# A mixture-of-experts loop: a turn of four experts instead of eight, and the down bias as a combination of its own

## The chip, the cores and the metric

One core of one Trainium2 chip runs the whole program. The metric is the device time of one execution in microseconds (us).

## The reference

One inference step of a decoder trunk of one layer, for 256 prompt tokens and 8 sample tokens (264 together), model width 1024, all in float32. Ahead of the part that changes stand a mixer and a cross-attention. Then comes a mixture of 32 experts, of which each token takes 4:

```python
def expert_ffn(xb, w1, b1, w2, b2):
    gu = xb @ w1 + b1                       # 1024 -> 2048
    gate, up = gu[:, :D_EXPERT], gu[:, D_EXPERT:]
    gate = jnp.minimum(gate, SWIGLU_LIMIT)
    up = jnp.clip(up, -SWIGLU_LIMIT, SWIGLU_LIMIT)
    glu = gate * jax.nn.sigmoid(gate * SWIGLU_ALPHA)
    return ((up + 1) * glu) @ w2 + b2       # 1024 -> 1024
```

The result of each expert is weighed with the token's gate and summed over the token's four experts, added to the residual, and a last RMSNorm follows. The down bias `b2` (`b_down`, 32 x 1024) thus enters a token's sum as its gates times the rows of `b_down`.

## The kernel before

The residual `resid` lies feature-major in SBUF, 8 tiles of 128 features x 264 tokens. After attention, router logits are ranked, and for each expert the tokens that chose it get ranks. An expert has 64 slots for tokens.

All weights come through `ring`, 12 slots of 1 MB. An expert's weights are 6 units of 2 MB, 2 slots each: units 0 to 3 gate/up, 4 and 5 down. SyncE issues them in order (L347, `expert_loads`); each issue waits until TensorE has used the unit that lay there, which is the same unit of the expert before. So the ring holds one expert, and the first expert's weights are in it before the loop.

The other engines run one loop each over the experts. In the kernel before, a turn of the loop does eight experts, so four turns (`end`, read from `iters`) do 32. Were an expert chosen by more than 64 tokens, all experts would be run again with the next 64 ranks; this input doesn't need it. For each expert TensorE does, in this order:
- the gate/up pass, L1170: 32 calls, each 64 slots x 512 columns, in two passes (64 records), in four groups that each wait for their unit
- for the first expert of a pair, the transposed gates of the pair (L1180) that ScalarE copies into `g_hot`
- two of four combination matmuls (L1145) into PSUM banks 6 and 7: `y_hot` (results of the pair of experts before, slots x features) times `g_hot` (gates, slots x tokens), 128 features a call. VectorE adds each to `resid` (L842)
- transposes of the gate/up result (L1200); VectorE adds the bias (L863) and does the SwiGLU with ScalarE (L868 to L876)
- the gather of the next pair's tokens (L1117)
- the other two combination matmuls
- the down pass, L1217, 32 records in two groups, whose result ScalarE copies to `y_hot` (L569, L570)

A pair's results are combined while the next pair is computed: four of the eight feature tiles in its first expert and four in its second. In the first pair of the first turn the half that is combined (`y_hot[:, 1]`, `g_hot[:, 1]`) is zero, from memsets of GpSimd. After the loop the last pair is combined (L1224), and the final norm follows.

The down bias: the gates of all 32 experts, transposed (L1131), are copied to `gate_t` (L836), and `b_down` is loaded into `bdn`, both with zeros in the other 96 rows. In the fifth and the sixth expert of a turn (`biased = j in (4, 5)`) an extra matmul, L1144, starts each combination:

```python
if biased:
    mm(ps[:, 6 + m % 2, 0:T], bdn[:, P * m:P * m + P], gate_t[:], start=True, stop=False)
mm(ps[:, 6 + m % 2, 0:T], y_hot[:, pair, P * m:P * m + P], g_hot[:, pair, :],
   start=not biased, stop=True).then_inc(c_filled, 1)
```

So that it counts once, GpSimd subtracts `gate_t` from itself at the end of each turn, and TensorE waits for that (`gates_zero`) ahead of the fifth expert. Zeroing ahead of the loop is counted by `late_zero` (five steps), for which ScalarE (ahead of the load of `bdn`), VectorE and TensorE wait.

Of the kernel before, what the change touches and what calls it, by code (L numbers as in the profile page):

```python
# [12 lines left out]
P = 128  # L13
D = 1024
# [7 lines left out]
NE = 32  # L22
# [51 lines left out]
def build(nc, x_t, mem_t, w_k, w_v, w_in, w_out, w_q, w_xo, kc, vc, w_gu, w_dn, params, ws_t,  # L74
# [3 lines left out]
    with ExitStack() as ctx:  # L78
# [112 lines left out]
        g_hot = view(sq_at, 2, T)  # L191
        gate_t = view(sq_at + 2 * T, T)
        bdn = view(sq_at + 3 * T, D)
        assert 3 * T + D <= KT * T

# [68 lines left out]
        tok_copied = sem("tok_copied")  # L264
        gates_zero = sem("gates_zero")
        late_zero = sem("late_zero")
# [57 lines left out]
        def _(sp):  # L324
# [42 lines left out]
            sp.wait_ge(iters_ready, 1)  # L367
            end = sp.value_load(iters[0:1, 0:1], min_val=4, max_val=20)
            with sp.If(end > 4):
                with sp.Fori(1, end >> 2) as again:  # L370
                    with sp.Fori(0, NE) as expert:
                        expert_loads(again * NE + expert, expert)
# [9 lines left out]
        def _(pool):  # L382
            counts = {}
            pool.sem_inc(gates_zero, 1)

# [38 lines left out]
            pool.wait_ge(sum_ready, 4)  # L424
            step(nc.gpsimd.memset(gate_t[:], 0.0), late_zero)
            step(nc.gpsimd.memset(bdn[:], 0.0), late_zero)
            step(nc.gpsimd.memset(g_hot[:, 1, :], 0.0), late_zero)
# [14 lines left out]
            pool.wait_ge(iters_ready, 1)  # L442
            end = pool.value_load(iters[0:1, 0:1], min_val=4, max_val=20)
            with pool.Fori(0, end) as it:
                for part in range(4):
                    pair = it * 4 + part
                    first = (pair + 1) & 15
                    pool.wait_ge(side_filled, pair * 3 + 1 + 1)
                    pool.wait_ge(p_built, pair + 2)
                    build_w(first, pair + 2)  # L450

                pool.wait_ge(c_filled, it * 32 + 24)
                nc.gpsimd.tensor_tensor(gate_t[:], gate_t[:], gate_t[:], ALU.subtract).then_inc(gates_zero, 1)


        @block.scalar
        def _(act):
# [85 lines left out]
            nc.scalar.activation(ex[:], ex[:], ACT.Exp).then_inc(ex_out, 1)  # L543
            act.wait_ge(late_zero, 5)
            act.dma_start(bdn[0:NE, :], b_down).then_inc(bdn_in, 16)

            act.wait_ge(iters_ready, 1)
            end = act.value_load(iters[0:1, 0:1], min_val=4, max_val=20)
            act.wait_ge(emptied, NG)
            with act.Fori(0, end) as it:  # L550
                for j in range(8):
                    e, i, pair, nxt = it * 8 + j, j % 4, it * 4 + j // 2, (j // 2 + 1) % 2
                    act.wait_ge(gu_done, e + 1)
                    act.wait_ge(t_done, e + 1)
                    nc.scalar.activation(gu_sb.rearrange("p (a b) -> p a b", a=2), ps[:, 0:2, :],  # L555
                                         ACT.Copy).then_inc(gu_copied, 1)
                    pos = pair * 3 + 2 * (j % 2)
                    if i % 2 == 0:
# [5 lines left out]
                    act.wait_ge(side_filled, pos + 2)  # L564
                    nc.scalar.activation(xg[:, nxt, 4 * (j % 2):4 * (j % 2) + 4, :], ps[:, 5, :].rearrange("p (a b) -> p a b", a=4),  # L565
                                         ACT.Copy).then_inc(side_copied, 1)
# [5 lines left out]
            for m in range(KT):  # L572
                act.wait_ge(c_added, end * 32 + m + 2)
                nc.scalar.activation(h_fm[:, m, :], resid[:, m, :], ACT.Square).then_inc(sq_ready, 1)
# [5 lines left out]
        def _(dve):  # L580
# [242 lines left out]
            link(nc.vector.tensor_reduce(nover, over, AX.X, ALU.add))  # L823
            TS(iters[:], nover[0:1, :], 4.0, 4.0, ALU.mult, ALU.add).then_inc(iters_ready, 1)
            dve.wait_ge(ex_out, 1)
# [5 lines left out]

            dve.wait_ge(late_zero, 5)
            for n in range(2):
                copy(xg[:, 0, 4 * n:4 * n + 4, :], filled(("ga", n)).rearrange("p (a b) -> p a b", a=4)).then_inc(emptied, 1)
                if n == 0:
                    copy(gate_t[0:NE, :], filled("gT", T)[0:NE]).then_inc(emptied, 2)  # L836
            dve.wait_ge(emptied, NG)
# [6 lines left out]
            dve.wait_ge(iters_ready, 1)  # L844
            end = dve.value_load(iters[0:1, 0:1], min_val=4, max_val=20)
            with dve.Fori(0, end) as it:
                expert0 = (it & 3) * 8
                for j in range(8):
                    e, i, pair = it * 8 + j, j % 4, it * 4 + j // 2
                    if i % 2 == 0:  # L850
# [10 lines left out]
                    for h in range(2):  # L861
                        bias = b_tiles[:, :, bass.ds(expert0 + j, 1), h, :].rearrange("p m a b -> p (a b) m")
# [14 lines left out]
                    for r in range(2, 4):  # L877
                        combine(e * 4 + r, 4 * (i % 2) + r)
            dve.wait_ge(c_added, end * 32 + 1)
            for m in range(KT):  # L880
                dve.wait_ge(c_filled, end * 32 + m + 1)
# [6 lines left out]
            dve.wait_ge(c_added, end * 32 + 8 + 1)  # L888
            for m in range(KT):
# [5 lines left out]
        def _(pe):  # L895
# [224 lines left out]

            pe.wait_ge(late_zero, 5)
            pe.wait_ge(tok_copied, 6)
# [3 lines left out]
            pe.wait_ge(iters_ready, 1)  # L1126
            end = pe.value_load(iters[0:1, 0:1], min_val=4, max_val=20)
            b = begin("gT")
# [7 lines left out]

            def combine(n, r, m, pair, biased=False):

                if r == 0:
                    pe.wait_ge(c_added, n + 1)  # L1140
                elif r >= 2:
                    pe.wait_ge(c_added, n + r - 1 + 1)
                if biased:
                    mm(ps[:, 6 + m % 2, 0:T], bdn[:, P * m:P * m + P], gate_t[:], start=True, stop=False)  # L1144
                mm(ps[:, 6 + m % 2, 0:T], y_hot[:, pair, P * m:P * m + P], g_hot[:, pair, :],  # L1145
                   start=not biased, stop=True).then_inc(c_filled, 1)

            with pe.Fori(0, end) as it:
                for j in range(8):
                    e, i, cur = it * 8 + j, j % 4, (j // 2) % 2  # L1150
                    twin = it * 4 + j // 2

# [9 lines left out]
                    for u in range(4):  # L1162
                        if j == 0 and u == 2:
                            pe.wait_ge(emptied, NG)
                        w = expert_unit(u)
                        for k in (2 * u, 2 * u + 1):
                            for n in range(2):
                                for h in range(2):
                                    at = SLOT * (k % 2) + D * h + 512 * n
                                    last = mm(ps[64 * h:64 * h + 64, n, :], xg[:, cur, k, SLOTS * (j % 2):SLOTS * (j % 2) + SLOTS],  # L1170
                                              w[:, at:at + 512], start=(k == 0), stop=(k == KT - 1))
                        last.then_inc(w_used if u < 3 else gu_done, 1)

                    pos = twin * 3 + 2 * (j % 2)
                    if i % 2 == 0:
# [12 lines left out]
                    if i == 2:  # L1188
                        pe.wait_ge(y_copied, twin * 2 + 1)
                    biased = j in (4, 5)  # L1190
                    if j == 4:
                        pe.wait_ge(gates_zero, it + 1)
                    for r in range(2):
                        combine(e * 4, r, 4 * (i % 2) + r, pair, biased)

# [9 lines left out]
                    pe.wait_ge(p_built, twin + 2)  # L1205
                    gather(ps[:, 5, :], j % 2).then_inc(side_filled, 1)
                    for r in range(2, 4):
                        combine(e * 4, r, 4 * (i % 2) + r, pair, biased)

                    pe.wait_ge(hid_ready, e + 1)  # L1210
                    pe.wait_ge(y_copied, e + 1)
                    for u in range(4, UNITS):
# [6 lines left out]
                        last.then_inc(w_used if u < UNITS - 1 else d_done, 1)  # L1219
            pe.wait_ge(y_copied, end * 8 + 1)  # L1220
            pe.wait_ge(c_added, end * 32 + 1)
            pe.wait_ge(side_copied, end * 12 + 1)
            for m in range(KT):
# [68 lines left out]
```

## Time and profile before

| | us |
|---|---|
| time, median of 3 runs | 1229.42 |
| lowest and highest of them | 1229.14, 1229.61 |
| the profiled execution's own time | 1230.66 |
| its span, first to last instruction | 1228.9 |
| TensorE busy, share of the span | 95% |
| VectorE, ScalarE, GpSimd busy | 23%, 14%, 3% |
| mean granted TensorE clock | 0.991 |

Profile views name engines PE (TensorE matmul), PEld (its weight loads), DVE (VectorE), ACT (ScalarE), POOL (GpSimd) and SP or SPq (SyncE and its DMA queue). L1170 is line 1170 of the kernel, xN a count of records. The chain of work is followed back from the last instruction, at each step to what released it; "issue" is time in which the engine waited for nothing that the profile shows. A row of groups by line has the operation, its shape, its count, then busy us and mean ns of one, then the idle time before it with what ended it. A row of stages has the stretch, its length, busy us of PE, PEld, DVE, ACT and POOL, then the granted TensorE clock as a share of full speed, the busy share of the DMA engines and GB/s. A row of DMA issues has the transfer, its count, its size and the median us from issue to landing. In a row of the timeline, start and length come first.

### The profile page before, as it was taken

To read this page: it belongs to the slowest core of one execution; us is meant where nothing else is said; L and a number is where in the kernel's file an instruction comes from. 1 tells how busy PE (TensorE), PEld (TensorE's weight loads), DVE (VectorE), ACT (ScalarE), POOL (GpSimd) and SP (SyncE) were. 2 spreads that over 40 slices of the span, in tenths; PEclk is the share of its full clock that TensorE was granted. 3 is DMA by queue.
4 is the path that set the end of the run, shared out by engine and by line. 5 is a ranking of instruction groups with operands and counts; after the bars stand their busy time and mean duration, and the time that the engine had idled before them with its cause. 6 is when DMAs were issued, how large, how long until landed. Compare 5 with 4: busy or idle time off the path is not lost.

```text
span 1228.9 us, 14979 instructions
## 1 busy us (share of the span) xinstructions
PE 1162.9 (95%) x5977; PEld 628.8 (51%) x5977; DVE 282.8 (23%) x608; ACT 166.0 (14%) x267; POOL 31.9 (3%) x68
## 2 busy tenths in 40 slices
PE   8999999999999999999999999999999899999995
PEld 7888887784444454444344434443444343434443
DVE  5114532342111122121111111111111111111115
ACT  2011011022111111111111111111111111111112
POOL 0000000010000000000000000000000000000000
PEclk9999999999999999999999999999999999999998
DMA  9963434948999999999999999999999999999991
GB/s 365 387 222 138 139 138 175 429 189 331 431 426 428 428 427 427 426 427 427 429 427 427 428 427 428 427 428 427 429 427 428 426 428 427 427 429 427 429 397 57
DMA packets 38703, 458.87 MB, mean 373 GB/s; under 512 B 5841, under 2 KB 6353, under 8 KB 7921
## 3 DMA queue, kind: packets, MB, share of 16 engines
q1 hardware_dynamic: 35712, 454.11, 88.1%
q10 hardware_dynamic: 2928, 3.80, 0.9%
q8 instruction: 54, 0.88, 0.3%
q14 instruction: 9, 0.07, 0.0%
HBM read 454.41 MB, written 3.23 MB: 372 GB/s over the span
## 4 chain that ended last, share of the span: by engine, by line
DMA 44%; PE 29%; DVE 3%; issue 1%; DVEq 0%; ACT 0%; SPq 0%; ACTq 0%
DMA ring<-in_w_gu 44%; PE ps L1170 19%; PE ps L1217 6%; PE ps L1145 1%; DVE arena L863 1%; PE ps L1200 1%; PE ps L1117 1%; DVE arena L873 1%; DVE arena L876 1%; PE ps L1144 0%; DVE arena L870 0%; DVE resid L890 0%; DVE resid L882 0%; DVE ssum L608 0%; PE ps L1180 0%
## 5 line engine op out<-in xcount | busy, mean ns | idle before, releaser
L1170 PE MATMUL ps<-ring,arena 128*64 128x512 f32 x2048 | 457.5, 599 | 36.7 <-DMA ring<-in_w_gu 29.2
L1170 PEld LDWEIGHTS ps<-ring,arena 128*64 128x64 f32 x2048 | 144.9, 138 | 343.8 <-issue 279.4
L1217 PE MATMUL ps<-ring,arena 128*64 128x512 f32 x1024 | 226.8, 595 | 6.3 <-DVE arena L876 6.3
L842 DVE TENSOR_TENSOR resid<-resid,ps 128x264 f32<-128x264 f32 x128 | 51.3, 426 | 722.4 <-PE ps L1145 722.4
L940 PE MATMUL ps<-arena,ring 128*128 128x264 f32 (+1 forms) x800 | 179.2, 386 | 1.4 <-issue 1.0
L940 PEld LDWEIGHTS ps<-arena,ring 128*128 128x128 f32 x800 | 151.6, 190 | 27.3 <-issue 1.6
L1217 PEld LDWEIGHTS ps<-ring,arena 128*64 128x64 f32 x1024 | 70.7, 137 | 146.9 <-issue 130.7
L1117 PE MATMUL ps<-arena 128*128 128x128 f32 x816 | 101.7, 281 | 0.0
L1117 PEld LDWEIGHTS ps<-arena 128*128 128x128 f32 x816 | 99.1, 197 | 0.0
L555 ACT ACTIVATE arena<-ps 128x1024 f32<-128x1024 f32 x32 | 32.8, 1024 | 446.2 <-PE ps L1170 446.2
L1145 PE MATMUL ps<-arena 128*128 128x264 f32 x256 | 72.6, 396 | 0.0
L569 ACT ACTIVATE arena<-ps 64x512 f32<-64x512 f32 x32 | 18.9, 590 | 249.4 <-PE ps L1217 249.4
L1145 PEld LDWEIGHTS ps<-arena 128*128 128x128 f32 x256 | 44.8, 190 | 15.2 <-issue 9.7
L863 DVE TENSOR_TENSOR arena<-ps,par 128x512 f32<-128x512 f32 x64 | 44.0, 688 | 25.9 <-PE ps L1200 25.9
L1200 PEld LDWEIGHTS ps<-ident,arena 128*128 128x128 f32 x256 | 34.7, 207 | 7.4 <-issue 6.3
L1200 PE MATMUL ps<-ident,arena 128*128 128x128 f32 x256 | 36.9, 287 | 1.4
L431 POOL TENSOR_TENSOR arena<-arena,gate 128x384 f32<-128x384 f32 x17 | 14.2, 833 | 879.1 <-PE ps L1180 873.0
L563 ACT ACTIVATE arena<-arena 128x512 f32<-128x512 f32 x32 | 20.2, 630 | 85.2 <-DVE arena L868 85.2
L967 PE MATMUL ps<-ring,arena 128*128 128x256 f32 x128 | 28.0, 379 | 0.0
L967 PEld LDWEIGHTS ps<-ring,arena 128*128 128x128 f32 x128 | 24.3, 190 | 3.3
L876 DVE TENSOR_TENSOR arena<-arena 128x512 f32<-128x512 f32 x32 | 22.2, 692 | 3.3
L565 ACT ACTIVATE arena<-ps 128x512 f32<-128x512 f32 x32 | 19.1, 597 | 27.6 <-PE ps L1117 27.6
(187 smaller groups left out, 433.5 us busy)
## 6 DMA issues: line engine op xcount, KB each, us to landing
ring<-in_w_gu SPq DMA_DIRECT2D x128, 2048.0 KB, 23.8
ring<-in_w_dn SPq DMA_DIRECT2D x64, 2048.0 KB, 20.4
ring<-in_w_in SPq DMA_DIRECT2D x10, 1024.0 KB, 27.2
ring<-in_kc SPq DMA_DIRECT2D x8, 1024.0 KB, 4.7
ring<-in_vc SPq DMA_DIRECT2D x8, 1024.0 KB, 4.8
ring<-in_w_v SPq DMA_DIRECT2D x4, 1024.0 KB, 22.7
ring<-in_w_out SPq DMA_DIRECT2D x4, 1024.0 KB, 4.9
ring<-in_w_q SPq DMA_DIRECT2D x4, 1024.0 KB, 4.8
```

The lines of the kernel that those rows point to most:

```text
L555: nc.scalar.activation(gu_sb.rearrange("p (a b) -> p a b", a=2), ps[:, 0:2, :], ACT.Copy).then_inc(gu_copied, 1)
L563: nc.scalar.activation(sig[:], tb[:, :, 0:SLOTS], ACT.Sigmoid, scale=ALPHA).then_inc(sig_ready, 1)
L842: TTN(resid[:, m, :], resid[:, m, :], ps[:, 6 + m % 2, 0:T], ALU.add).then_inc(c_added, 1)
L863: TTN(both[:, :, h, :].rearrange("p (b m) s -> p b m s", b=2), turned[:, :, h, :].rearrange("p (b m) s -> p b m s", b=2), bc(bias, 3, [P, ...
L876: TTN(hid[:], up_v, sig[:], ALU.mult).then_inc(hid_ready, 1)
L940: last = mm(b[:, 0:width], w[:, k, P * (m % 2):P * (m % 2) + P], source(k), start=(k == 0), stop=(k == KT - 1))
L967: last = mm(b[:, 0:256], mem[:, k, P * t:P * t + P], w[:, k, :], start=(k == 0), stop=(k == KT - 1))
L1117: last = mm(b[:, P * part:P * part + P], h_tok[:, t, first:first + ROWS_GU * (P - 1) + 1:ROWS_GU], p_hot[:, t, :], start=(t == 0), stop=(t ...
L1145: mm(ps[:, 6 + m % 2, 0:T], y_hot[:, pair, P * m:P * m + P], g_hot[:, pair, :], start=not biased, stop=True).then_inc(c_filled, 1)
L1170: last = mm(ps[64 * h:64 * h + 64, n, :], xg[:, cur, k, SLOTS * (j % 2):SLOTS * (j % 2) + SLOTS], w[:, at:at + 512], start=(k == 0), stop= ...
L1200: last = turn(ps[:, 2 + f // 4, P * (f % 4):P * (f % 4) + P], gu_sb[:, first:first + ROWS_DN * (P - 1) + 1:ROWS_DN], ident[:])
L1217: last = mm(ps[64 * h:64 * h + 64, 4, :], hid[:, k, :], w[:, at:at + 512], start=(k == 0), stop=(k == KT - 1))
```

## The change

A turn does four experts, and there are eight turns (the counts that start from `iters` or from the turn are adapted on each engine, so that the same 32 experts are run). The extra matmuls, `gate_t`, `bdn`, two of five zeroing steps and GpSimd's subtraction with its wait are gone. `b_down` is loaded into the first 32 rows of `y_hot[:, 1]` and the gates go to the first 32 rows of `g_hot[:, 1]`, so the combination of the first pair, which combined zeros, now adds the bias.

```diff
-        gate_t = view(sq_at + 2 * T, T)
-        bdn = view(sq_at + 3 * T, D)
...
-            TS(iters[:], nover[0:1, :], 4.0, 4.0, ALU.mult, ALU.add).then_inc(iters_ready, 1)
+            TS(iters[:], nover[0:1, :], 8.0, 8.0, ALU.mult, ALU.add).then_inc(iters_ready, 1)
...
-            pool.sem_inc(gates_zero, 1)
...
-            step(nc.gpsimd.memset(gate_t[:], 0.0), late_zero)
-            step(nc.gpsimd.memset(bdn[:], 0.0), late_zero)
             step(nc.gpsimd.memset(g_hot[:, 1, :], 0.0), late_zero)
...
             with pool.Fori(0, end) as it:
-                for part in range(4):
-                    pair = it * 4 + part
+                for part in range(2):
+                    pair = it * 2 + part
...
-                pool.wait_ge(c_filled, it * 32 + 24)
-                nc.gpsimd.tensor_tensor(gate_t[:], gate_t[:], gate_t[:], ALU.subtract).then_inc(gates_zero, 1)
...
-            act.wait_ge(late_zero, 5)
-            act.dma_start(bdn[0:NE, :], b_down).then_inc(bdn_in, 16)
+            act.wait_ge(late_zero, 3)
+            act.dma_start(y_hot[0:NE, 1, :], b_down).then_inc(bdn_in, 16)
...
-                    copy(gate_t[0:NE, :], filled("gT", T)[0:NE]).then_inc(emptied, 2)
+                    copy(g_hot[0:NE, 1, :], filled("gT", T)[0:NE]).then_inc(emptied, 2)
...
-                if biased:
-                    mm(ps[:, 6 + m % 2, 0:T], bdn[:, P * m:P * m + P], gate_t[:], start=True, stop=False)
                 mm(ps[:, 6 + m % 2, 0:T], y_hot[:, pair, P * m:P * m + P], g_hot[:, pair, :],
-                   start=not biased, stop=True).then_inc(c_filled, 1)
+                   start=True, stop=True).then_inc(c_filled, 1)
...
             with pe.Fori(0, end) as it:
-                for j in range(8):
-                    e, i, cur = it * 8 + j, j % 4, (j // 2) % 2
-                    twin = it * 4 + j // 2
+                for i in range(4):
+                    e, cur = it * 4 + i, i // 2
+                    twin = it * 2 + i // 2
...
-                    biased = j in (4, 5)
-                    if j == 4:
-                        pe.wait_ge(gates_zero, it + 1)
```

The loops of ScalarE and VectorE change as TensorE's does. SyncE's loop had one expert a turn and keeps it.

## Rows read from the trace of the kernel before

**Rows 1.** The page, part 2: GB/s moved in 40 equal slices.

```profile
GB/s 365 387 222 138 139 138 175 429 189 331 431 426 428 428 427 427 426 427 427 429 427 427 428 427 428 427 428 427 429 427 428 426 428 427 427 429 427 429 397 57
```

**Rows 2.** The page, part 4: the chain of work by line, shares of the span.

```profile
DMA ring<-in_w_gu 44%; PE ps L1170 19%; PE ps L1217 6%; PE ps L1145 1%; DVE arena L863 1%; PE ps L1200 1%; PE ps L1117 1%; DVE arena L873 1%; DVE arena L876 1%; PE ps L1144 0%; DVE arena L870 0%; DVE resid L890 0%; DVE resid L882 0%; DVE ssum L608 0%; PE ps L1180 0%
```

**Rows 3.** The chain in order of time, before the first branch: start, length, what.

```profile
331.67 13.73 PE ps L1170 x64
...
359.01 13.73 PE ps L1170 x64
...
386.22 13.73 PE ps L1170 x64
...
415.03 13.73 PE ps L1170 x64
...
443.32 13.76 PE ps L1170 x64
...
457.24 24.30 DMA ring<-in_w_gu
...
481.59 3.65 PE ps L1170 x16
```

**Rows 4.** The same view, from the first branch to the last landing.

```profile
498.72 2.49 issue
...
501.21 15.49 PE ps L1170 x64
...
541.44 3.68 PE ps L1170 x16
...
719.14 3.65 PE ps L1170 x16
...
736.27 2.28 issue
...
738.55 15.65 PE ps L1170 x64
...
807.56 3.68 PE ps L1170 x16
...
955.88 3.65 PE ps L1170 x16
...
973.02 2.70 issue
...
975.72 15.46 PE ps L1170 x64
...
1015.82 3.68 PE ps L1170 x16
...
1193.01 3.65 PE ps L1170 x16
```

**Rows 5.** Stages, last three: granted clock, DMA share, GB/s. Behind branches 1, 3.

```profile
501.00:504.50 3.50, 3.29 (x10) 1.03 (x12) 0.00 (x0) 0.26 (x1) 0.00 (x0) 0.53 1.03 435
...
952.00:972.00 20.00, 18.40 (x100) 8.90 (x98) 5.54 (x11) 2.25 (x3) 0.00 (x0) 1.00 1.01 428
...
972.00:992.00 20.00, 17.30 (x75) 5.68 (x72) 0.00 (x0) 3.26 (x4) 0.00 (x0) 0.91 1.00 425
```

**Rows 6.** DMA issues: 382 to 388 us, 495 to 500 us; then SyncE's timeline.

```profile
ring<-in_w_dn SPq DMA_DIRECT2D x2, 2048.0 KB, 16.0
...
ring<-in_w_dn SPq DMA_DIRECT2D x2, 2048.0 KB, 22.2
...
506.56 10.63 SPq L347 DMA_DIRECT2D ring<-in_w_gu  x4
```

**Rows 7.** DMA queues, 304 to 1193 us: the instruction queue, packets, MB, share.

```profile
q8 instruction: 40, 0.66, 0.3%
```

**Rows 8.** Groups by line: bias matmuls; one GpSimd memset.

```profile
L1144 PE MATMUL ps<-arena 128*128 128x264 f32 x64 | 20.3, 399 | 0.0
...
L426 POOL MEMSET arena<- 128x1024 f32 x1 | 1.0, 957 | 0.1
```

More of the change, by code:

```diff
@@ L191, in build @@
         g_hot = view(sq_at, 2, T)
-        gate_t = view(sq_at + 2 * T, T)
-        bdn = view(sq_at + 3 * T, D)
-        assert 3 * T + D <= KT * T
+        assert 2 * T <= KT * T
         ps = ctx.enter_context(nc.psum_tensor("ps", [P, 8, 512], F32))
@@ L264, in build @@
         tok_copied = sem("tok_copied")
-        gates_zero = sem("gates_zero")
         late_zero = sem("late_zero")
@@ L367, in _ @@
             sp.wait_ge(iters_ready, 1)
-            end = sp.value_load(iters[0:1, 0:1], min_val=4, max_val=20)
-            with sp.If(end > 4):
-                with sp.Fori(1, end >> 2) as again:
+            end = sp.value_load(iters[0:1, 0:1], min_val=8, max_val=40)
+            with sp.If(end > 8):
+                with sp.Fori(1, end >> 3) as again:
                     with sp.Fori(0, NE) as expert:
@@ L442, in _ @@
             pool.wait_ge(iters_ready, 1)
-            end = pool.value_load(iters[0:1, 0:1], min_val=4, max_val=20)
+            end = pool.value_load(iters[0:1, 0:1], min_val=8, max_val=40)
             with pool.Fori(0, end) as it:
-                for part in range(4):
-                    pair = it * 4 + part
+                for part in range(2):
+                    pair = it * 2 + part
                     first = (pair + 1) & 15
@@ L543, in _ @@
             nc.scalar.activation(ex[:], ex[:], ACT.Exp).then_inc(ex_out, 1)
-            act.wait_ge(late_zero, 5)
-            act.dma_start(bdn[0:NE, :], b_down).then_inc(bdn_in, 16)
+            act.wait_ge(late_zero, 3)
+            act.dma_start(y_hot[0:NE, 1, :], b_down).then_inc(bdn_in, 16)
             act.wait_ge(iters_ready, 1)
-            end = act.value_load(iters[0:1, 0:1], min_val=4, max_val=20)
+            end = act.value_load(iters[0:1, 0:1], min_val=8, max_val=40)
             act.wait_ge(emptied, NG)
             with act.Fori(0, end) as it:
-                for j in range(8):
-                    e, i, pair, nxt = it * 8 + j, j % 4, it * 4 + j // 2, (j // 2 + 1) % 2
+                for i in range(4):
+                    e, pair, nxt = it * 4 + i, it * 2 + i // 2, 1 - i // 2
                     act.wait_ge(gu_done, e + 1)
@@ L556, in _ @@
                                          ACT.Copy).then_inc(gu_copied, 1)
-                    pos = pair * 3 + 2 * (j % 2)
+                    pos = pair * 3 + 2 * (i % 2)
                     if i % 2 == 0:
@@ L564, in _ @@
                     act.wait_ge(side_filled, pos + 2)
-                    nc.scalar.activation(xg[:, nxt, 4 * (j % 2):4 * (j % 2) + 4, :], ps[:, 5, :].rearrange("p (a b) -> p a b", a=4),
+                    nc.scalar.activation(xg[:, nxt, 4 * (i % 2):4 * (i % 2) + 4, :], ps[:, 5, :].rearrange("p (a b) -> p a b", a=4),
                                          ACT.Copy).then_inc(side_copied, 1)
@@ L572, in _ @@
             for m in range(KT):
-                act.wait_ge(c_added, end * 32 + m + 2)
+                act.wait_ge(c_added, end * 16 + m + 2)
                 nc.scalar.activation(h_fm[:, m, :], resid[:, m, :], ACT.Square).then_inc(sq_ready, 1)
@@ L830, in _ @@
             TTN(gate[:], ex[:], bc(gsum, 2, [P, TT, NE]), ALU.mult).then_inc(gate_ready, 1)
-            dve.wait_ge(late_zero, 5)
+            dve.wait_ge(late_zero, 3)
             for n in range(2):
@@ L844, in _ @@
             dve.wait_ge(iters_ready, 1)
-            end = dve.value_load(iters[0:1, 0:1], min_val=4, max_val=20)
+            end = dve.value_load(iters[0:1, 0:1], min_val=8, max_val=40)
             with dve.Fori(0, end) as it:
-                expert0 = (it & 3) * 8
-                for j in range(8):
-                    e, i, pair = it * 8 + j, j % 4, it * 4 + j // 2
+                expert0 = (it & 7) * 4
+                for i in range(4):
+                    e, pair = it * 4 + i, it * 2 + i // 2
                     if i % 2 == 0:
@@ L861, in _ @@
                     for h in range(2):
-                        bias = b_tiles[:, :, bass.ds(expert0 + j, 1), h, :].rearrange("p m a b -> p (a b) m")
+                        bias = b_tiles[:, :, bass.ds(expert0 + i, 1), h, :].rearrange("p m a b -> p (a b) m")
                         TTN(both[:, :, h, :].rearrange("p (b m) s -> p b m s", b=2),
@@ L878, in _ @@
                         combine(e * 4 + r, 4 * (i % 2) + r)
-            dve.wait_ge(c_added, end * 32 + 1)
+            dve.wait_ge(c_added, end * 16 + 1)
             for m in range(KT):
-                dve.wait_ge(c_filled, end * 32 + m + 1)
+                dve.wait_ge(c_filled, end * 16 + m + 1)
                 TTN(resid[:, m, :], resid[:, m, :], ps[:, (0, 1, 2, 3, 5, 6, 7, 4)[m], 0:T], ALU.add).then_inc(c_added, 1)
@@ L887, in _ @@
             inverse(5, rstd[:, 0, :])
-            dve.wait_ge(c_added, end * 32 + 8 + 1)
+            dve.wait_ge(c_added, end * 16 + 8 + 1)
             for m in range(KT):
@@ L1119, in gather @@
                 return last
-            pe.wait_ge(late_zero, 5)
+            pe.wait_ge(late_zero, 3)
             pe.wait_ge(tok_copied, 6)
@@ L1126, in _ @@
             pe.wait_ge(iters_ready, 1)
-            end = pe.value_load(iters[0:1, 0:1], min_val=4, max_val=20)
+            end = pe.value_load(iters[0:1, 0:1], min_val=8, max_val=40)
             b = begin("gT")
@@ L1135, in _, with combine @@
             pe.wait_ge(emptied, NG - 1)
-            def combine(n, r, m, pair, biased=False):
+            def combine(n, r, m, pair):
                 if r == 0:
@@ L1142, in combine @@
                     pe.wait_ge(c_added, n + r - 1 + 1)
-                if biased:
-                    mm(ps[:, 6 + m % 2, 0:T], bdn[:, P * m:P * m + P], gate_t[:], start=True, stop=False)
                 mm(ps[:, 6 + m % 2, 0:T], y_hot[:, pair, P * m:P * m + P], g_hot[:, pair, :],
-                   start=not biased, stop=True).then_inc(c_filled, 1)
+                   start=True, stop=True).then_inc(c_filled, 1)
             with pe.Fori(0, end) as it:
-                for j in range(8):
-                    e, i, cur = it * 8 + j, j % 4, (j // 2) % 2
-                    twin = it * 4 + j // 2
+                for i in range(4):
+                    e, cur = it * 4 + i, i // 2
+                    twin = it * 2 + i // 2
                     def expert_unit(n):
@@ L1162, in _ @@
                     for u in range(4):
-                        if j == 0 and u == 2:
+                        if i == 0 and u == 2:
                             pe.wait_ge(emptied, NG)
@@ L1169, in _ @@
                                     at = SLOT * (k % 2) + D * h + 512 * n
-                                    last = mm(ps[64 * h:64 * h + 64, n, :], xg[:, cur, k, SLOTS * (j % 2):SLOTS * (j % 2) + SLOTS],
+                                    last = mm(ps[64 * h:64 * h + 64, n, :], xg[:, cur, k, SLOTS * (i % 2):SLOTS * (i % 2) + SLOTS],
                                               w[:, at:at + 512], start=(k == 0), stop=(k == KT - 1))
                         last.then_inc(w_used if u < 3 else gu_done, 1)
-                    pos = twin * 3 + 2 * (j % 2)
+                    pos = twin * 3 + 2 * (i % 2)
                     if i % 2 == 0:
@@ L1189, in _ @@
                         pe.wait_ge(y_copied, twin * 2 + 1)
-                    biased = j in (4, 5)
-                    if j == 4:
-                        pe.wait_ge(gates_zero, it + 1)
                     for r in range(2):
-                        combine(e * 4, r, 4 * (i % 2) + r, pair, biased)
+                        combine(e * 4, r, 4 * (i % 2) + r, pair)
                     pe.wait_ge(gu_copied, e + 2)
@@ L1205, in _ @@
                     pe.wait_ge(p_built, twin + 2)
-                    gather(ps[:, 5, :], j % 2).then_inc(side_filled, 1)
+                    gather(ps[:, 5, :], i % 2).then_inc(side_filled, 1)
                     for r in range(2, 4):
-                        combine(e * 4, r, 4 * (i % 2) + r, pair, biased)
+                        combine(e * 4, r, 4 * (i % 2) + r, pair)
                     pe.wait_ge(hid_ready, e + 1)
@@ L1219, in _ @@
                         last.then_inc(w_used if u < UNITS - 1 else d_done, 1)
-            pe.wait_ge(y_copied, end * 8 + 1)
-            pe.wait_ge(c_added, end * 32 + 1)
-            pe.wait_ge(side_copied, end * 12 + 1)
+            pe.wait_ge(y_copied, end * 4 + 1)
+            pe.wait_ge(c_added, end * 16 + 1)
+            pe.wait_ge(side_copied, end * 6 + 1)
             for m in range(KT):
```

## The prediction

> **What bounds the kernel now.** I read the page first. Its GB/s line stands at 426 to 431 in every slice from the eleventh to the last but two [rows 1]: from about 307 us on, the weights of the experts stream at one level. The chain of work says the same by line: 44% of the span is the landing of `in_w_gu` [rows 2]. So the second view was the chain in order of time. In its first part [rows 3] a row "PE ps L1170 x64" is one expert's gate/up pass, and TensorE runs the 3rd expert (331.67) to the 7th (443.32) back to back without waiting for a load, because the ring was full when the loop began. From 457.24 on, the step that ends last is a DMA of 24.3 us, and the 8th expert's last gate/up group (x16) starts only as it lands, at 481.59. In the second part [rows 4] more such groups start at a landing: those of experts 10 (541.44), 16 (719.14), 19 (807.56), 24 (955.88), 26 (1015.82) and 32 (1193.01); the chain has the others between, one an expert. From the 8th to the 32nd, one expert takes (1193.01 - 481.59)/24 = 29.64 us of streaming. TensorE's own work on an expert, read where it never waits, is 359.01 - 331.67 = 27.34 us or 386.22 - 359.01 = 27.21 us [rows 3]. The DMA stream bounds this stage, and TensorE has 2.3 us to spare for each expert. The share of busy time (95% for TensorE) hides that.
>
> After the landing at 1193.0 come 35.9 us that are the kernel's tail: last down projection, last combination, final norm. The program writes the same instructions there before and after.
>
> **A turn's end.** The loop branches back three times in this profile, at 498.72, 736.27 and 973.02, each shown as "issue", a time in which TensorE waits for nothing else: 2.49, 2.28 and 2.70 us. The gate/up pass behind it takes 15.49, 15.65 and 15.46 us, where the passes of rows 3 take 13.73 [rows 3, 4]. The granted clock explains that part: it is 0.53 over the first 3.5 us behind the first branch [rows 5], nearly all of it at 1.2 GHz instead of 2.4, after an engine that had stood still for 2.5 us. A turn's end thus costs TensorE 17.98 - 13.73 = 4.25, 17.93 - 13.73 = 4.20 and 18.16 - 13.73 = 4.43 us, 4.3 in the mean.
>
> **The change, part by part.**
>
> Turns: eight instead of four, so seven branches back instead of three. The four that are new stand after the 4th, 12th, 20th and 28th expert. On TensorE that adds 4 x 4.3 = 17.2 us.
>
> Bias matmuls: in each old turn the fifth and sixth experts had an extra matmul before each of four combination matmuls, 32 calls in all, 64 records of 399 ns [rows 8] (two passes a call). What one turn's share costs is read off the chain: the biased experts of the first turn take 415.03 - 386.22 = 28.81 and 443.32 - 415.03 = 28.29 us, the plain ones before them 27.34 and 27.21, so 1.47 + 1.08 = 2.55 us [rows 3]. (The records' own time is more; plain experts wait for VectorE's bias add and products, which the extra matmuls covered.) Four turns: 10.2 us removed from TensorE. Its balance over the stage is 17.2 - 10.2 = 7.0 us more work.
>
> Does any of it reach the end? A new turn asks of TensorE 2 x (27.34 + 27.21) + 4.3 = 113.4 us, and the stream gives a turn 4 x 29.64 = 118.6. The cover is 5.2 us a turn; were it gone, each turn would cost what exceeds it. The recovery can be seen: behind the branches at 498.72 and 973.02, the next expert's last group already waits for its landing again, and behind the one at 736.27 the second next does [rows 4]. The new last branch has four experts behind it, so at the last of them TensorE waits for the landing at 1193 as before. I take 0 for TensorE's balance.
>
> The other way a late TensorE can hurt is to give ring slots back so late that the DMA queue runs dry. SyncE issues a unit when TensorE has used the one before it in the slot. Ahead of the new first branch (386.2 us), the last issues take 16.0 us to land, and ahead of an old one 22.2 us [rows 6]. The next unit goes out when the following pass has used its first: at the old branch that is 506.56 [rows 6], 7.8 us after it (498.72). The queue holds work for 16 us at the new first branch, so 8 us are to spare, and more at the later ones. No gap, term 0.
>
> What the stream itself loses at a turn's end isn't quite nothing. In the 20 us behind the third branch it moved 425 GB/s, against 428 in the 20 us ahead of it [rows 5]: 20 x 3/428 = 0.14 us. The spacing of landings gives a coarser bound. Over stretches without a branch it is (719.14 - 541.44 + 955.88 - 807.56 + 1193.01 - 1015.82)/17 = 29.60 us. Across the three branches the landings come 59.85, 88.42 and 59.94 us apart, which is +0.65, -0.38 and +0.74 against 2, 3 and 2 times 29.60; and the stretch behind the third has 29.53, so part of it is given back. The bounds for one branch are -0.38 and +0.74. I take 0.1 us, by the bytes, which are the nearest to what is wanted (time lost for good, not a phase): 4 x 0.1 = +0.4 us.
>
> The down bias as a combination: the first expert and the second already combined the second half of `y_hot` with that of `g_hot`, with both zero. Now these hold `b_down` and the gates in 32 rows. Same matmuls, same VectorE adds, no new wait, 0. The load of `b_down` keeps its queue (ScalarE's), its size and its place behind the same ACT instructions; the copy of the gates keeps its shape. The waits on `late_zero` lose two memsets of GpSimd, one of 0.96 us [rows 8] and one of a quarter of its width, so the bounds are -1.2 us (both on the path) and 0. I take 0: router results that end later, on VectorE and TensorE, lead to the first pass, and no memset stands in the chain by line [rows 2]. GpSimd's wait for `c_filled` and its subtraction at each turn's end go, and with them TensorE's wait on `gates_zero`; no row shows TensorE held there. VectorE, ScalarE and GpSimd branch twice as often too, each while it waits for TensorE's next pass. 0.
>
> Sum against the profiled execution: 1230.66 (span 1228.9, 1.8 around it) + 0 + 0 + 0.4 = 1231.1. That execution is 1.2 us above the median of the runs, so against the median 1229.4 + 0.4 = 1229.8.
>
> The Trainium skill has a rule that speaks against this change: "Runtime: NRT & Kernel Launch", section "Instruction fetch mechanics", says that a taken branch leaves the sequential prefetch and stalls the engine for a fetch of the target, and that unrolling is preferred for it. The trace agrees, with 2.3 to 2.7 us at each branch. The sum has the new stalls under the stream; by the rule taken alone they would reach the end, with the 1236.4 of rival 3.
>
> **The rivals.**
> 1. The shorter body stays on hand. Half the instructions may fit into what TensorE keeps, so that the branch neither stalls nor fetches. For it: nothing in the trace, which has no short loop; against: the stage fetched 40 blocks over 889 us [rows 7] at a steady need, none of them kept for the next turn. If so, the stream gets back 0.66 MB/427 GB/s = 1.5 us, and the three old branches' mean excess, 3 x 0.34 = 1.0 us: 1229.4 - 1.5 = 1227.9 for the first alone, 1226.9 for both. 0.22; a third of it beyond 0.2%.
>  The same section of that page gives TensorE's instruction memory 128 KiB and also calls it a window of two blocks; by the first figure the new body would fit and the old one would not, by the second neither. No run here shows which.
> 2. Slower, by the stream: each new turn's end delays the landings for good by what the worst of the old ones shows, 0.74 us. Place: the units issued in the late pass. 4 x 0.74 = 3.0 us, 1232.4. It decides over 0.2% from 2.5/4 = 0.6 us a branch. For it: two of three branches; against: the third and the GB/s. 0.08.
> 3. TensorE's balance reaches the end: 1229.4 + 7.0 = 1236.4. It needs a turn's end of more than 118.6 - 109.1 = 9.5 us, or a stream faster than 28.4 us per expert. 0.02.
> 4. The removed matmuls were on the path: 1229.4 - 10.2 = 1219.2. Against it are the landings of rows 4. 0.02.
>
> **How the numbers follow.** Forecast 1229.8 with 0.66. A measurement of this kernel can tell about 0.2%, 2.5 us. Faster by more: 0.07 (of rival 1) + 0.02 = 0.09. Slower: 0.08 + 0.02 = 0.10. Within: 0.81. The range goes from 1227.2, which takes in most of rival 1, to 1231.6: the forecast with the mean excess of 0.34 at each branch would be 1230.8, and some of rival 2 lies above that.
>
> **What would show it.** Right: seven stretches of "issue" of 2 to 3 us on TensorE, the new ones near 386, 620, 857 and 1094, the granted clock low behind each; the record of the bias matmuls gone; landings still 29.6 us apart and the last at 1193, the tail 35.9. Rival 1: no such stretches, and far fewer instruction blocks than 40 in the stage. Rival 2: the last landing 2 to 3 us later. I am wrong if the first gate/up pass or the stream's level of 428 GB/s moves by itself.

## The result

The changed kernel takes 1222.3 us, median of 4 runs (1222.12 to 1222.94), against 1229.5 before (1229.14 to 1229.74): a ratio of 0.9943 with a 95% interval of 0.9930 to 0.9955, 7.2 us faster. The profile of the changed kernel, the lines that answer to rows 1, 2 and 7 (its line numbers are up to 14 lower: the gate/up pass is L1159, the down pass L1203):

```profile
span 1220.6 us, 14896 instructions
...
GB/s 365 399 217 139 140 138 172 428 197 322 430 426 428 428 430 427 430 427 429 428 428 429 428 427 430 427 429 430 428 428 428 428 428 429 428 429 428 428 428 74
...
DMA ring<-in_w_gu 54%; PE ps L1159 15%; PE ps L1203 3%; DVE arena L854 1%; PE ps L1186 1%; PE ps L1134 1%; PE ps L1108 0%; DVE arena L867 0%; DVE arena L864 0%; DVE resid L881 0%; DVE arena L861 0%; DVE resid L873 0%; DVE ssum L599 0%; DVE rstd L607 0%; SPq L344 0%
...
q8 instruction: 16, 0.26, 0.1%
```

and its DMA queues between 304 and 1185 us, packets, MB, share (q1 carries the weights), then q1 of before in the same window:

```profile
q1 hardware_dynamic: 25915, 377.42, 100.6%
q8 instruction: 3, 0.05, 0.0%
```

```profile
q1 hardware_dynamic: 25806, 375.91, 100.3%
```

The stream of weights has nearly the same level, 428 GB/s; the kernel before moved 1.51 MB less in these 881 us, which is 3.5 us of streaming. But between 304 and 1185 us only 3 instruction blocks were fetched, where the kernel before fetched 40, and in the whole run 16, where it fetched 54 (its page has "q8 instruction: 54, 0.88, 0.3%"). The chain in order of time, first of after, then the one row of before that rows 3 and 4 lack, its first gate/up pass:

```profile
275.65 13.88 PE ps L1159 x64
...
377.90 7.09 PE ps L1203 x32
...
384.99 13.73 PE ps L1159 x64
...
450.86 3.68 PE ps L1159 x16
...
480.22 3.68 PE ps L1159 x16
...
509.59 3.68 PE ps L1159 x16
...
538.95 3.68 PE ps L1159 x16
...
715.14 3.68 PE ps L1159 x16
...
1184.97 3.65 PE ps L1159 x16
```

```profile
276.88 13.88 PE ps L1170 x64
```

The new turn's end behind the 4th expert lies between 377.90 + 7.09 = 384.99 and the pass that begins at 384.99: it takes no time that the chain can show, and no "issue" of 2 us stands anywhere in it. The later turns' ends could hide from the chain, which runs over the landings there; but TensorE's waits between 300 and 1190 us have no row of issue either. The last of the blocks is fetched at 363.8 us, in the first turn, and none later. From the 7th expert (450.86) on, every last gate/up group starts 29.36 us after the one before it, without the irregular steps of before. Where the 8.3 us between the two spans lie:

| stretch | before | after | difference |
|---|---|---|---|
| start to first gate/up pass | 276.88 | 275.65 | 1.23 |
| first pass to last group of the 8th expert | 204.71 | 204.57 | 0.14 |
| from there to the last group of the 32nd | 711.42 | 704.75 | 6.67 |
| from there to the end | 35.89 | 35.63 | 0.26 |

The 1.23 us in the first row aren't of the change: they are there at 10 us already, ahead of all that it touches (the last part of `in_mem_t` landed 1.2 us later in the profiled execution of before, which lies 1.2 us above its own median). Another 0.26 lies in the tail, whose instructions are the same. The change made 6.8 us, nearly all in the stage where the stream of weights ends last. The 3.5 us above are half of that. The other half shows in how the stream ends. Stages of 2 us around the end of the stream, three of before and three of after:

```profile
1194.00:1196.00 2.00, 2.00 (x12) 0.64 (x10) 0.00 (x0) 0.00 (x0) 0.00 (x0) 1.00 0.54 229
...
1196.00:1198.00 2.00, 1.89 (x9) 0.82 (x6) 0.58 (x2) 1.02 (x1) 0.00 (x0) 1.00 0.52 221
...
1198.00:1200.00 2.00, 2.00 (x18) 2.00 (x19) 0.92 (x3) 0.00 (x0) 0.00 (x0) 1.00 0.50 213
```

```profile
1186.00:1188.00 2.00, 2.00 (x12) 0.60 (x10) 0.00 (x0) 0.00 (x0) 0.00 (x0) 1.00 1.00 426
...
1190.00:1192.00 2.00, 2.00 (x18) 2.00 (x19) 0.92 (x3) 0.00 (x0) 0.00 (x0) 1.00 1.00 426
...
1192.00:1194.00 2.00, 2.00 (x18) 1.97 (x18) 1.93 (x4) 0.72 (x2) 0.00 (x0) 1.00 0.39 164
```

The column ahead of GB/s is the busy share of the 16 DMA engines. Before, from 1194 us, the share is a half (0.54, 0.52, 0.50) for another 7 us or so. After, it is 1.00 to 1192 us, and all stop soon behind that. A mean share of a half doesn't say by itself that half of the engines are done, but the single packets that the trace keeps do: before, 16 packets of weights are under way at every moment up to 1193 us, 8 from 1196 to 1199 us, and the last ends at 1202.3. After, it is 16 at 1192 us, and the last ends at 1194.3. The bytes of the last units wait at a late half of the engines.

### The profile page after: what moved, and what is told of

It reads as the page before. It is cut to its first block, busy times and chain, and to the rows that moved or that the text cites. A ratio compares the mean times of both kernels' runs of the same rounds, so it can differ in the third digit from the quotient of the medians.

```text
span 1220.6 us, 14896 instructions
## 1 busy us (share of the span) xinstructions
PE 1148.4 (94%) x5913; PEld 615.3 (50%) x5913; DVE 281.4 (23%) x608; ACT 176.2 (14%) x275; POOL 28.2 (2%) x62
## 4 chain that ended last, share of the span: by engine, by line
DMA 54%; PE 20%; DVE 3%; issue 1%; ACT 0%; SPq 0%; DVEq 0%; ACTq 0%
DMA ring<-in_w_gu 54%; PE ps L1159 15%; PE ps L1203 3%; DVE arena L854 1%; PE ps L1186 1%; PE ps L1134 1%; PE ps L1108 0%; DVE arena L867 0%; DVE arena L864 0%; DVE resid L881 0%; DVE arena L861 0%; DVE resid L873 0%; DVE ssum L599 0%; DVE rstd L607 0%; SPq L344 0%
## 5 line engine op out<-in xcount | busy, mean ns | idle before, releaser
L1159 PE MATMUL ps<-ring,arena 128*64 128x512 f32 x2048 | 456.2, 595 | 41.6 <-DMA ring<-in_w_gu 41.6
L1159 PEld LDWEIGHTS ps<-ring,arena 128*64 128x64 f32 x2048 | 143.7, 137 | 348.1 <-issue 269.8
L1203 PE MATMUL ps<-ring,arena 128*64 128x512 f32 x1024 | 226.8, 595 | 8.4 <-DVE arena L867 8.4
L1203 PEld LDWEIGHTS ps<-ring,arena 128*64 128x64 f32 x1024 | 70.7, 137 | 149.6 <-issue 127.9
```

The costliest lines, as they stand in the source:

```text
L1203: last = mm(ps[64 * h:64 * h + 64, 4, :], hid[:, k, :], w[:, at:at + 512], start=(k == 0), stop=(k == KT - 1))
```

## The experiments

Each kernel's stream is read from its first gate/up pass to the last gate/up group of the 32nd expert ("stretch"), which leaves out the start and the tail, in the one execution that was profiled; the blocks are those between 304 and 1185 us. "Instructions" are TensorE's in one turn, counted in the program to about 1%: four for a matmul call in float32 (two weight loads, two passes), two for a transpose, one for each register or semaphore operation.

| kernel | time, median us | instructions | blocks | stretch, us |
|---|---|---|---|---|
| before | 1229.5 | 2314 | 40 | 916.13 |
| after | 1222.3 | 1143 | 3 | 909.32 |
| turn4_bias | 1224.8 | 1176 | 3 | 911.35 |
| turn8_nobias | 1229.3 | 2281 | 40 | 916.16 |
| te8_others4 | 1229.6 | 2281 | 40 | 915.93 |
| te4_others8 | 1223.1 | 1143 | 3 | 909.61 |
| body2153 | 1228.3 | 2153 | 36 | 915.66 |
| body1897 | 1224.6 | 1897 | 33 | 916.30 |
| body1641 | 1217.0 (one execution) | 1641 | 5 | 908.52 |
| body1385 | 1216.5 (one execution) | 1385 | 4 | 908.53 |
| packet16k | 1240.1 | 1143 | 3 | 926.27 |
| packets1k | 1229.7 | 1143 | 3 | 916.73 |
| packets16x16k | 1312.3 | 1143 | 3 | 997.28 |
| spread16x16k | 1275.4 | 1143 | 3 | 960.31 |
| spread1k | 1226.1 | 1143 | 3 | 912.35 |

**Which part of the change made it.** First the two halves apart. The kernel before with turns of four, its bias matmuls kept:

```diff
-                for j in range(8):
-                    e, i, cur = it * 8 + j, j % 4, (j // 2) % 2
+                for i in range(4):
...
+                    e, cur = it * 4 + i, i // 2
...
-                    biased = j in (4, 5)
+                    biased = i in (0, 1)
```

> The kernel before with a turn of four experts; the extra bias matmuls stay (now in the first two experts of each of eight turns, twice as many as before, all but the first turn's adding zeros). Theory S (the short body stays in TensorE's instruction store, so the blocks are no longer fetched and the stream of weights is not delayed): 1222.3 us, no stretch of issue behind a turn, about 16 instruction blocks in the whole run, landings 29.37 us apart. Rival B (the removed matmuls made the gain): 1229.5 or more. Rival P (the earlier memsets made part of it): 1223.5.

Measured: 1224.8 us, ratio 0.9956 (0.9939 to 0.9973), 3 blocks, no issue at a turn's end. Though it has twice the bias matmuls of before, it is 4.8 us faster. The other half, bias as a combination and turns of eight:

```diff
-            with pe.Fori(0, end) as it:
-                for i in range(4):
-                    e, cur = it * 4 + i, i // 2
...
+            with pe.Fori(0, end >> 1) as it:
+                for j in range(8):
+                    i = j % 4
+                    e, cur = it * 8 + j, i // 2
```

(and so on each engine)

> The changed kernel with a turn of eight experts again on all engines; the down bias stays a combination of its own. Theory S: the blocks are fetched again, 50 or so, with 2.3 to 2.7 us of issue at three turns' ends, and 1229.5 us. Rival B: 1222.3. A mixture would lie between.

Measured: 1229.3 us, ratio 0.9995 (0.9986 to 1.0005). The removed matmuls are worth nothing at eight experts a turn; rival B falls, and so does rival P, since this kernel has the earlier memsets. The length of the turn makes the gain.

turn4_bias stays 2.0 us behind after in the stretch, which the theory had not asked for. Its first expert shows where: with two more matmul passes on each combination it takes 305.66 - 276.70 = 28.96 us, where after has 303.22 - 275.65 = 27.57. At 301 to 303 us, before the first down unit is given back, the DMA engines run dry for longer than in the kernel before (stage row of turn4_bias, then of before):

```profile
301.00:303.00 2.00, 2.00 (x12) 0.66 (x10) 0.00 (x0) 0.00 (x0) 0.00 (x0) 1.00 0.44 180
```

```profile
301.00:303.00 2.00, 2.00 (x12) 0.57 (x8) 0.00 (x0) 0.00 (x0) 0.00 (x0) 1.00 0.89 279
```

That is the one place seen at which TensorE's work reaches the stream: the ring is full at the start, and TensorE gives the slots of the down units back only with the first down pass. The first expert is 1.39 us longer, which would be most of the 2.0; for the rest no run shows a cause. The change moved no work there (the first expert had no bias matmul before either).

**Which engine.** Eight experts a turn on TensorE only, and the reverse:

> The changed kernel with a turn of eight experts on TensorE alone; VectorE, ScalarE and GpSimd keep four. Theory S, since TensorE has nearly all instructions: 1229, about 50 blocks. If the other engines' blocks matter: 1224 to 1227.

> The changed kernel with a turn of eight experts on VectorE, ScalarE and GpSimd, and four on TensorE. Theory S: 1222.3, about 16 blocks. If the other engines' blocks matter: 1224 to 1227.

Measured: 1229.6 (ratio 0.9998, 0.9988 to 1.0007) and 1223.1 (0.9946, 0.9929 to 0.9962). From te8_others4 the instruction queue in the stage, then the chain's rows; its turns' ends are those of before:

```profile
q8 instruction: 40, 0.66, 0.3%
```

```profile
276.69 13.88 PE ps L1160 x64
...
498.65 2.51 issue
...
736.21 2.25 issue
...
972.80 2.45 issue
...
1192.62 3.65 PE ps L1160 x16
```

So TensorE's body decides, and the branches of the other three engines cost nothing that can be measured.

**The length in instructions, or the number of experts?** Four kernels have eight experts a turn on TensorE and leave work out of the loop, so that a turn has fewer instructions. The first:

```diff
-                    for t in range(TT):
+                    tiles = TT if begun else 2
+                    for t in range(tiles):
...
```

> Eight experts a turn on TensorE, four on the others, and in the loop the gather leaves out the third tile of tokens (the sample tokens): 2153 instead of 2281 instructions of TensorE in a turn. If the number of instructions in a turn decides: still fetched, about 50 blocks and 1229 us. If the removed work decides: 1222 to 1226.

Measured: 1228.3 us, 36 blocks, and issue of 2.15, 2.24 and 2.10 us at the turns' ends. The next leaves two of three tiles out of the gather and two of eight `k` out of the down pass:

> Eight experts a turn on TensorE, four on the others; in the loop the gather leaves out two of three tiles of tokens, and the down pass two of eight tiles of hidden features: 1897 instructions of TensorE in a turn. If what decides is whether the turn's instructions fit, and the limit lies between this and 2153: about 16 blocks, no issue at a turn's end and 1222 us. If it lies lower, or if eight experts a turn are the cause by something else: about 40 blocks and 1228 us.

Measured: 1224.6 us. This looked like the limit, and was not. 33 blocks were fetched, and the stretch is 916.30 us, as before. The profiled execution (1226.9 us) is 3.8 us shorter than that of before outside the stretch: its first gate/up pass starts 2.2 us earlier (274.71 for 276.88), and 1.8 us are missing behind the last landing, where it has less down work. The other five executions are 2 us shorter still (1224.5 to 1225.0), and no trace says where, so the stretch of 916.30 is that of the slowest one. The blocks are what decides. TensorE still stands at this kernel's three turns' ends, though the chain doesn't pass there; from its waits between 300 and 1190 us (total, times, longest):

```profile
PE ps L1161 <- issue: 5.0, 3, 2.3
```

The median alone would have misled. The last two leave out more: six of eight `k` in the down pass, and then also two of eight in the gate/up pass:

> As the kernel with 1897 instructions in a turn of TensorE, but the down pass in the loop keeps only two of its eight tiles of hidden features: 1641 instructions in a turn. Its tail is shorter by the missing down work, so the stream is to be read alone, from the first gate/up pass to the last landing of gate/up weights. If the limit of what stays lies above 1641: few blocks in the stage and 909.5 us for that stretch. If it lies below: about 30 blocks and 915.5 us or more.

> The same, and the gate/up pass in the loop leaves out two of eight tiles of features: 1385 instructions in a turn. If the limit lies above 1385: few blocks and 909.5 us from the first gate/up pass to the last landing. If it lies between 1143 (the changed kernel) and this: about 25 blocks and 914 us or more.

Measured: 908.52 and 908.53 us of stretch, 5 and 4 blocks. The instruction queue in the stage, first of body1897, then of body1641, and the ends of the stretch in body1641's chain:

```profile
q8 instruction: 33, 0.54, 0.3%
```

```profile
q8 instruction: 5, 0.08, 0.0%
```

```profile
274.38 13.96 PE ps L1161 x64
...
1182.90 3.65 PE ps L1161 x16
```

With eight experts a turn and 1641 instructions the stream is as undisturbed as with four and 1143. The last of its blocks is fetched at 467.4 us, in the first turn, and TensorE's waits have no row of issue. What decides is that the instructions of TensorE's turn fit; the limit lies between 1641 and 1897 of them.

**Why a block costs the stream more than its bytes.** The blocks' 0.6 MB are 1.4 us of stream, and the gain is 6.8. Into the changed kernel, where nothing is fetched, ScalarE was made to load 16 KB an expert that nobody uses:

```diff
                     act.wait_ge(g_ready, e + 1)
+                    act.wait_ge(extra_in, e * 16 + 1)
+                    act.dma_start(arena[0:1, sq_at + 2 * T:sq_at + 2 * T + 4096],
+                                  w_gu[0, 0, 0:2, :].rearrange("(a p) n -> a (p n)", a=1)).then_inc(extra_in, 16)
...
```

> The changed kernel plus one load of 16 KB for each expert, a single row into one partition, issued by ScalarE beside the stream of weights; the data are used by nobody. It imitates an instruction block, 32 of them. If a block delays one of the 16 DMA engines and a unit of weights counts as landed only when the last engine is done: each load costs 0.6 us or more if they all fall on one engine, 1222.3 + 19 = 1241 us or more, and about 1222.3 + 32 x 0.18 = 1228 if they fall as the blocks did. If only the bytes count: 32 x 16 KB/428 GB/s = 1.2 us, 1223.5.

Measured: 1240.1 us, 17.8 more than the changed kernel. Chain rows, then stages behind the end of the stream:

```profile
275.76 13.88 PE ps L1163 x64
...
962.40 3.68 PE ps L1163 x16
...
992.37 3.68 PE ps L1163 x16
...
1202.03 3.65 PE ps L1163 x16
```

```profile
1202.00:1204.00 2.00, 1.97 (x10) 0.77 (x12) 0.00 (x0) 0.00 (x0) 0.00 (x0) 1.00 0.06 25
...
1204.00:1214.00 10.00, 9.64 (x58) 6.20 (x56) 5.01 (x10) 2.25 (x3) 0.00 (x0) 1.00 0.05 21
```

Steps of 992.37 - 962.40 = 29.97 us, 0.6 us longer for each 16 KB. And behind the last landing of gate/up weights the busy share is 0.06 and 0.05: one of the 16 engines works alone. By the trace's packets it does so from 1198.3 to 1211.4 us, 13 us. A delay on one engine isn't made good, since the other engines don't take over its rows; it adds up, and a unit has landed only when the latest engine is done.

A block isn't quite such a load, as the packets show. Each of the loads' rows of 16 KB took 0.61 us, like a packet of weights (0.61 in the median). In the kernel before, each of the 40 blocks in the stage took 1.01 to 1.10 us (mean 1.06), and each had a packet of weights of 1.07 to 1.16 us (mean 1.11) right behind it, where 0.61 is usual. A block thus takes 1.06 + 0.50 = 1.56 us of one engine's time.

The same bytes over 16 rows should then cost their bytes (the change in short, not as code):

```diff
-  arena[0:1, ... + 4096]   w_gu[0, 0, 0:2, :] as 1 row of 16 KB
+  arena[0:16, ... + 256]   the same as 16 rows of 1 KB
```

> The same with the same 16 KB for each expert, cut into 16 rows of 1 KB for 16 partitions, which can fall on all engines. By bytes, and by the theory of the late engine alike: 1223.5 to 1224.5 us. If small loads cost the stream for another reason (their issue, a change of queue): as much as with the single row.

Measured: 1229.7 us, so 7.4 us more than the changed kernel in place of 1.2. It costs less than half of the single row, but six times its bytes; the expectation missed. Sixteen rows of 16 KB, to see whether all engines together cost what one does:

> The changed kernel plus one load of 256 KB for each expert: sixteen rows of 16 KB into sixteen partitions, sixteen times the bytes of the single row. If the stream is as late as its latest DMA engine, and the rows fall on all engines, this costs what the single row cost, 0.60 us for each expert (landings 29.97 us apart, 1240 us), with all engines ending together. If rows share few engines, or if each load's bytes add up at one place: 1260 us or more.

Measured: 1312.3 us, (997.28 - 909.32)/32 = 2.75 us an expert, where the single row made (926.27 - 909.32)/32 = 0.53 by the same measure. The expectation missed again. Both loads went to 16 neighbouring partitions, so these went to every eighth instead (`arena[0:128:8, ...]`):

> As the kernel with sixteen rows of 16 KB for each expert, but the rows go to every eighth of the 128 partitions, not to the first sixteen. If neighbouring partitions share the way into SBUF and that is what made the sixteen rows cost 2.8 us an expert: now the bytes alone, 0.6 us an expert, landings 29.97 us apart and 1241 us. If the sixteen rows fall on few engines whatever their partitions: still above 1300.

> As the kernel with sixteen rows of 1 KB for each expert, but to every eighth partition. If the price of 0.21 us an expert came from the neighbouring partitions: 1223.5 to 1224.5 us. If it is what a small packet costs each engine: 1229.7 as with neighbouring ones.

Measured: 1275.4 us, (960.31 - 909.32)/32 = 1.59 us an expert, and 1226.1 us, (912.35 - 909.32)/32 = 0.09. The neighbouring partitions made 1.16 of the 2.75 us, and 0.14 of the 0.23 that the 1 KB rows cost. With the rows apart, the small load costs twice its bytes (0.09 for 0.04), and the large one still 1.0 us more than its 0.6. The packets show it too: a row of 16 KB that took 0.61 us alone took 1.55 us in the mean when sixteen went to neighbouring partitions, and 1.03 when they went to every eighth. So rows that run at once slow each other beyond their bytes; which resource they share was not found.

## Why the prediction was wrong, point by point

- **What bounds the kernel** was right. The stream of weights ends last from the 7th or 8th expert on, and the bias matmuls were free: turn8_nobias is at 0.9995 of before. TensorE's balance was put at 0 in the sum, and it didn't reach the end. Rivals 3 and 4 are out.
- **What a turn's end costs TensorE** was right for the turns of eight (te8_others4 has 2.51, 2.25, 2.45 us) and wrong for the new ones. The step that failed is "The four that are new ... adds 4 x 4.3 = 17.2 us": it carried the price of one branch to another, whose target is 1143 instructions back and not 2314. With it went the forecast's only term, +0.4 us of stream for four more branches (4 x 0.1), where the stream gained 6.8. Seven stretches of issue were foretold, and there is none. The 17.2 us themselves cost the forecast nothing, as the sum hid them anyway.
- **Rival 1 came true**, and got 0.22. I wrote that nothing in the trace spoke for it. But 40 blocks over 32 experts [rows 7] say only that a long turn is fetched anew each time; they say nothing on a short one, and I took them as evidence against. The Trainium skill, "Runtime: NRT & Kernel Launch", section "Instruction fetch mechanics", has both readings, 128 KiB (2048 instructions) for TensorE and a window of two blocks of 256. Here the measurement decides against the second, since 1641 instructions stayed; and it puts the limit between 1641 and 1897, somewhat below the first.
- **The price of rival 1 was the second fault, and the one that put the result out of the range.** The term is "the stream gets back 0.66 MB/427 GB/s = 1.5 us". It took the 16 engines for one pipe. The measured gain is 6.8 us for 37 blocks, 0.18 us a block, five times its bytes at 0.04. By the packets a block takes 1.56 us of one engine. The early eight engines end 917.3 us after the first gate/up pass in the mean, as all sixteen do in the changed kernel (917.5), so the blocks fell on the other eight: 40 x 1.56/8 = 7.8 us for each of these, which end 7.3 us later. The signs were in the profile: the chain's landings came 29.60 us apart in stretches without a branch, and I had no term for why the weights' 12.58 MB took 29.60 and not the 29.4 that 428 GB/s give. I took 29.64 as the stream's own pace. The view that would have shown it, the stages behind 1194 us with half the engines idle, stands in no row of the prediction; only rows 1 have a trace of it, 397 GB/s in the last slice but one, where the changed kernel has 428.
- **The excess of landings across branches** (+0.65, -0.38, +0.74) was taken for a price of the branch. But the chain of before has landings 29.88 and 29.97 us apart where no branch stands (29.36 after), and packet16k is late at every step with 3 blocks in the stage. What the engines carry beside the weights delays the landings. A branch is where blocks lie close together (body1897 fetched one at 496.1 and one at 502.4 us, with a step of 30.43 us across them), and no run has a branch that fetches without its blocks, so a price of the branch apart from them is neither shown nor needed.
- **Memsets and `late_zero`** at 0: right; turn8_nobias has them and is as before.

The price also holds across kernels. The mean end of the late eight engines lies 7.3 us behind that of the early eight with 40 blocks in the stage (before), 7.0 with 36 (body2153) and 6.5 with 33 (body1897); blocks x 1.56/8 gives 7.8, 7.0 and 6.4. That the stretch is nearly the same for the three (915.7 to 916.3 us) is then no contradiction: it goes by the latest engine and not by the mean, and in body1897 two engines end some 1.1 us behind the other six. What stays open is why the blocks fall on one half of the engines, and why a block takes 1.06 us and the packet behind it 1.11 where a row of weights of the same size takes 0.61.

## What to carry to other kernels

In a stage that the DMA engines bound, ask what else the engines carry, TensorE's own instructions first: look at the instruction queue's packets within the stage, and count the instructions of a loop's turn. Here a turn of up to 1641 of them on TensorE was fetched once, one of 1897 or more again and again; unrolling beyond that saved no time at the branches and cost the stream. Judge such traffic by the engine that is latest, not by bytes over total bandwidth: look at the busy share of the DMA engines in short stages just behind the end of a stream, and if it falls to a half or a sixteenth there instead of to zero, the load is uneven.

## What the runs showed of the hardware

- A taken branch whose target is at most 1641 instructions of TensorE back cost nothing that the chain or TensorE's waits show (the chain of after has the next pass at the end of the last, at 384.99), while one over 2153 or more cost 2.1 to 2.7 us. At 1897 the blocks were fetched, and TensorE stood three times, 5.0 us in all (1.1 to 2.3), off the chain.
- An instruction block of 16 KB took 1.06 us of a DMA engine beside the stream, and the packet of weights behind it 1.11 us; a packet of weights of 16 KB takes 0.61. The 40 blocks of before left eight engines 7.3 us behind the other eight.
- Each load of 16 KB in one row made the stream 0.6 us later, each time (29.97 us for 29.36), for 16 KB/428 GB/s = 0.04 us of bytes.
- Sixteen rows of 16 KB an expert beside the weights cost 2.75 us to 16 neighbouring partitions and 1.59 us to every eighth; their bytes alone make 0.6.
